# Four weight slots of one 128-column tile and a longer stretch of turns in a hybrid encoder block

## Chip, cores and metric

One core of a Trainium2 chip. The metric is the device time of one execution in microseconds; lower is better. A step, below, is always one expert of one head for 128 tokens (see the kernel).

## Reference

One encoder layer on x of 512 tokens by 2048 features, all in float32, then a final RMSNorm:

```python
h = rmsnorm(x); proj = h @ w_in          # q, k, v, og, two decay gates, glu, ga, gb
yA = (rmsnorm_heads(gla(q, k, v, decay)) * silu(og)) @ w_o
yB = silu(layernorm(depthwise_conv31(glu_in * sigmoid(glu_gate)))) @ w_pw2
x  = x + (sigmoid(ga) * yA + sigmoid(gb) * yB) @ w_out
h2 = rmsnorm(x)                          # PEER: 8 heads, top 16 of 128*128 experts each
x  = x + sum_k softmax_k * gelu(u_tab[idx_k] . h2) * v_tab[idx_k]
```

PEER reads, for each token, head and chosen expert, one row of u_tab and one of v_tab (8 KB each): 512 x 8 x 16 x 2 rows, 1.07 GB. The weights are 16 MiB for each 2048 x 2048 matrix, read once for each group of token blocks that is computed together.

## The kernel before

**Blocks and stages.** The tokens are four blocks of 128. Stage A (to 1303 us of the span) computes the linear attention of all 512 tokens and then everything of block 0 up to its expert indices. Stage B works off the experts of blocks 0 and 1 on VectorE while TensorE does the rest of blocks 1, 2 and 3 beside it. Later stages work off the experts of blocks 2 and 3, with the products of v_tab rows on TensorE.

**Steps.** Stage B is one unrolled list of 256 steps (L1464; 16 units of 16). In each, `dot` (L1301) multiplies a gathered u row with the tokens and `add_row` (L1309) adds a gathered v row, two steps late. GpSimd issues both gathers of a step (L584, L588; 1 MiB each, two buffers for u, four for v) when `dot` and `add_row` free a buffer. ScalarE makes the weight of a step in `expert` (L763). After its dot, each step does its share of the side work in `beside(s)` (L1390 on VectorE, L801 on ScalarE), at step numbers written out by hand (L81 to L101): a piece of side work can't come earlier on VectorE than its step, and a step can't go on until TensorE has delivered what the piece reads.

**Turns.** Steps 0 to 67 carry eight turns, one for each pair of channel tiles (`TURN_AT`, L81): four of ten steps, four of seven. A turn begins with `glu1_take` (L1319), which reads two projections from TensorE, tile by tile (L1327), and then spreads 62 operations of the convolution over its steps (`conv1`, L1332, L1343). In the first four turns TensorE computes four output-gate tiles (`og1`) and the four projections of the next turn (`glu1`), all of 384 columns; in the last four it computes two pairs of gate and value for block 1 (`ma1`, 128 columns) and the next turn's `glu1`. Behind the turns come the gates of the second branch (`GB_AT`, 66), the layer norm (`XC_AT` 71 to `SILU2_AT` 85), the pointwise projection (`PW_AT` 83), the output projection (`RES1_AT` 93 to 99), the second norm (100), and the queries of block 1 (`QUERY1_AT` 105, a head every two steps). From step 130 (`M2_AT`) `merge2` (L1378, L1385) takes a pair of gate and value for blocks 2 and 3 every four steps, 16 times.

**Weights.** SyncE loads them in the order of use with `load` (L484). `wring` has two slots; a load is a slab of 256 output columns, 2 MiB (or two half slabs for v and w_out). Before a load it waits on `w_used`. TensorE waits for the landing in `slab_ready`, computes the slab, and gives the slot back with a drain:

```python
            def slab_used():
                pe.drain().then_inc(w_used, 1)
```

So slab n+2 is issued when slab n has been computed. `tiles` (L1742) computes 2 x 16 matmuls of a slab into one bank, `project` (L1638) 16 matmuls of one tile, `project_out` (L1800) the half slabs of w_out. A float32 matmul shows as two records in the profile.

Of the kernel before, what the change touches and what calls it, by code (L numbers as in the profile page):

```python
# [5 lines left out]
P = 128  # L6
# [8 lines left out]
T = 512  # L15
# [19 lines left out]
WQ, WK, WV, WOG, WGLU, WGATE, WGA, WGB = 0, 4, 8, 16, 24, 32, 40, 48  # L35
OGK = 6144
# [14 lines left out]
SLAB = 4096  # L51
HEAD_SLABS = 4

SB_GLU0 = HEADS * HEAD_SLABS
SB_OG0 = SB_GLU0 + 16
SB_MA0 = SB_OG0 + 8
SB_MB0 = SB_MA0 + 16
SB_OUT0 = SB_MB0 + 16
SB_WQ0 = SB_OUT0 + 8
SB_GLU1 = SB_WQ0 + PH  # L60
SB_OG1 = SB_GLU1 + 2
SB_MA1 = SB_OG1 + 16
SB_MA1_LAST = SB_MA1 + 18
SB_GB1 = SB_MA1_LAST + 4
SB_PW1 = SB_GB1 + 8
SB_OUT1 = SB_PW1 + 8
SB_WQ1 = SB_OUT1 + 8
SB_MA2 = SB_WQ1 + PH
SB_MB2 = SB_MA2 + 16
SB_OUT2 = SB_MB2 + 16  # L70
SB_WQ2 = SB_OUT2 + 8
# [21 lines left out]
QUERY1_AT = 105  # L93
# [51 lines left out]
def hybrid_block(nc, x, norm1_g, w_in, w_gk, gk_f_w, gk_f_b, gk_b_w, gk_b_b, onorm_g, w_o, conv_w, conv_b,  # L145
                 ln_g, ln_b, w_pw2, w_out, norm2_g, w_q, keys, u_tab, v_tab, final_g, out):
    def slab(w, at):

        return w[bass.ds(at, 1)].rearrange("a p f -> p (a f)")

    def half_slab(w, at, s):

        return w[bass.ds(at, 2), :, s * (SLAB // 2):(s + 1) * (SLAB // 2)].rearrange("j p f -> p j f")

    ctx = ExitStack()
    with ctx:
# [25 lines left out]
        wring = sb("wring", [P, 2 * SLAB])  # L182
# [168 lines left out]
        w_in_slot = [sem("w_slot0"), sem("w_slot1")]  # L351
# [104 lines left out]
        def w_slot(n):  # L456

            return view(wring, (n % 2) * SLAB, KT, 256)

        def w_slot_half(n):  # L460

            return view(wring, (n % 2) * SLAB, 2, KT // 2, 256)

        def slot_all(n):

            return wring[:, (n % 2) * SLAB:(n % 2 + 1) * SLAB]

        def slot_halves(n):

            return slot_all(n).rearrange("p (j f) -> p j f", j=2)  # L470

        def by_half(bank):

            return bank.rearrange("p (j c) -> p j c", j=2)


        @block.sync
        def _(sp):
# [5 lines left out]
            def load(n, i, per, dst, src):  # L484

                hold(sp, w_used, i * per + (n + 1), sp_passed)
                sp.dma_start(dst, src).then_inc(w_in_slot[n % 2], 16)

            with sp.Fori(0, HEADS) as h:
                load(0, h, HEAD_SLABS, slot_all(0), slab(w_in, h + WQ))  # L490
                load(1, h, HEAD_SLABS, slot_all(1), slab(w_in, h + WK))
                for s in range(2):
                    load(2 + s, h, HEAD_SLABS, slot_halves(s), half_slab(w_in, h * 2 + WV, s))

            def pair_loads(first, w_gate, o_gate, w_val, o_val):
                with sp.Fori(0, KT // 2) as i:
                    load(first, i, 2, slot_all(0), slab(w_gate, i + o_gate))
                    load(first + 1, i, 2, slot_all(1), slab(w_val, i + o_val))

            def slab_loads(first, w, o, count=PH):  # L500
                with sp.Fori(0, count // 2) as i:
                    for s in range(2):
                        load(first + s, i, 2, slot_all(s), slab(w, i * 2 + (o + s)))

            def out_loads(first):
                with sp.Fori(0, 4) as g:
                    for s in range(2):
                        load(first + s, g, 2, slot_halves(s), half_slab(w_out, g * 2, s))

            pair_loads(SB_GLU0, w_in, WGATE, w_in, WGLU)  # L510
            slab_loads(SB_OG0, w_in, WOG)
            pair_loads(SB_MA0, w_in, WGA, w_o, 0)
            pair_loads(SB_MB0, w_in, WGB, w_pw2, 0)
            out_loads(SB_OUT0)
            slab_loads(SB_WQ0, w_q, 0)

            load(SB_GLU1, 0, 2, slot_all(0), slab(w_in, WGATE))
            load(SB_GLU1 + 1, 0, 2, slot_all(1), slab(w_in, WGLU))
            with sp.Fori(0, 4) as j:
                for s in range(2):  # L520
                    load(SB_OG1 + s, j, 4, slot_all(s), slab(w_in, j * 2 + (WOG + s)))
                load(SB_OG1 + 2, j, 4, slot_all(0), slab(w_in, j + (WGATE + 1)))
                load(SB_OG1 + 3, j, 4, slot_all(1), slab(w_in, j + (WGLU + 1)))
            with sp.Fori(0, 3) as j:
                for a in range(2):
                    load(SB_MA1 + 2 * a, j, 6, slot_all(0), slab(w_in, j * 2 + (WGA + a)))
                    load(SB_MA1 + 2 * a + 1, j, 6, slot_all(1), slab(w_o, j * 2 + a))
                load(SB_MA1 + 4, j, 6, slot_all(0), slab(w_in, j + (WGATE + 5)))
                load(SB_MA1 + 5, j, 6, slot_all(1), slab(w_in, j + (WGLU + 5)))
            for a in range(2):  # L530
                load(SB_MA1_LAST + 2 * a, 0, 4, slot_all(0), slab(w_in, WGA + 6 + a))
                load(SB_MA1_LAST + 2 * a + 1, 0, 4, slot_all(1), slab(w_o, 6 + a))
            slab_loads(SB_GB1, w_in, WGB)
            slab_loads(SB_PW1, w_pw2, 0)
            out_loads(SB_OUT1)
            slab_loads(SB_WQ1, w_q, 0)
# [3 lines left out]
            out_loads(SB_OUT2)  # L540
            slab_loads(SB_WQ2, w_q, 0)
# [418 lines left out]
        def _(dve):  # L960
# [503 lines left out]
            for U in range(2 * PH):  # L1464
                topk = None
                if U >= PH - 1:
                    head = U - (PH - 1)
                    topk = parts_beside(topk_1(head) if head < PH else topk_2(0), 1)
# [117 lines left out]
        def _(pe):  # L1586
# [11 lines left out]
            def slab_ready(n, i=None, per=0):  # L1598

                if i is None:  # L1600
                    pe.wait_ge(w_in_slot[n % 2], 16 * (n // 2 + 1))
                else:
                    pe.wait_ge(w_in_slot[n % 2], i * (8 * per) + 16 * (n // 2 + 1))


            pe.sem_inc(w_used, 2)
# [28 lines left out]
            def project(slot, m, act_in, bank, done, lo=0, hi=T):  # L1635

                for k in range(KT):
                    last = M(ps[bank][:, 0:hi - lo], w_slot(slot)[:, k, m * P:m * P + P], act_in[:, k, lo:hi],  # L1638
                             start=k == 0, stop=k == KT - 1)
                last.then_inc(done, 1)  # L1640
                return last


            with pe.Fori(0, HEADS) as h:
                for s in range(2):
                    slab_ready(s, h, HEAD_SLABS)
                    for m in range(MT):
                        project(s, m, hT, 2 * s + m, q_mm)
                    pe.drain().then_inc(w_used, 1)
# [8 lines left out]
                for s in range(2):  # L1658
                    slab_ready(2 + s, h, HEAD_SLABS)
                    for k in range(KT // 2):  # L1660
                        kk = s * (KT // 2) + k
                        for b in range(NB):
                            last = M(by_half(ps[b][:]), hT[:, kk, b * P:b * P + P], w_slot_half(s)[:, :, k, :],  # L1663
                                     start=kk == 0, stop=kk == KT - 1)
                            if kk == KT - 1:
                                last.then_inc(v_mm, 1)
                    pe.drain().then_inc(w_used, 1)
# [69 lines left out]
            def tiles(slot, act_in, bank, lo, hi, done):  # L1737

                w = hi - lo
                for m in range(2):  # L1740
                    for k in range(KT):
                        last = M(ps[bank][:, m * w:(m + 1) * w], w_slot(slot)[:, k, m * P:m * P + P],  # L1742
                                 act_in[:, k, lo:hi], start=k == 0, stop=k == KT - 1)
                last.then_inc(done, 1)

            def slab_used():
                pe.drain().then_inc(w_used, 1)

            def pairs(name, first, val_in, lo, hi, base=0):
                p = pair[name]  # L1750
                with pe.Fori(0, KT // 4) as i:
                    for m in range(2):
                        pe.wait_ge(p["use"], i * 2 + (base + m + 1))
                        slab_ready(first + 2 * m, i, 4)
                        tiles(0, hT, 4 + 2 * m, lo, hi, p["gate"])
                        slab_used()
                        slab_ready(first + 2 * m + 1, i, 4)
                        tiles(1, val_in, 5 + 2 * m, lo, hi, p["val"])
                        slab_used()
# [3 lines left out]
            def og0_slab(n):  # L1763
                slab_ready(SB_OG0 + n)
                pe.wait_ge(og0["used"], n + 1)
                tiles(n % 2, hT, n % 4, 0, P, og0["mm"])
                slab_used()
# [22 lines left out]
            def project_out(i, first, lhs, nb, bank0, out):  # L1790

                for g in range(2):
                    for s in range(2):
                        slab_ready(first + 2 * g + s, i, 4)
                        for k in range(KT // 2):
                            kk = s * (KT // 2) + k
                            for b in range(nb):
                                if kk == 0:
                                    pe.wait_ge(out["free"], i * (2 * nb) + (g * nb + b + 1))
                                last = M(by_half(ps[bank0 + g * nb + b][:]), lhs(kk, b), w_slot_half(s)[:, :, k, :],  # L1800
                                         start=kk == 0, stop=kk == KT - 1)
# [227 lines left out]
```

## Time and profile before

| | us |
|---|---|
| median of 3 runs | 4702.01 |
| lowest and highest | 4693.57, 4707.21 |
| the profiled execution | 4691.23 |
| its span, first to last instruction | 4689.5 |
| TensorE busy | 3759.9 (80%) |
| VectorE busy | 2744.8 (59%) |
| GpSimd busy | 1409.5 (30%) |
| moved by DMA | 1530.74 MB, mean 326 GB/s |

Durations come from the one profiled execution, whose own time lies 10.8 us under the median. 1.7 us of it lie outside the span. TensorE's granted clock over the span was 0.927 of full speed.

### The profile page before, as it was taken

The numbers are of one execution on the slowest core, as the hardware profiler recorded it, in microseconds if no ns is written. First come the engines' busy times: TensorE is split into PE (matmuls) and PEld (weight loads), VectorE is DVE, ScalarE is ACT, GpSimd is POOL, SyncE is SP. The second block draws the span as 40 slices with busy tenths as digits, with TensorE's granted clock in tenths as the row PEclk, the third lists the DMA queues.
The fourth block names the chain that finished last, engine by engine and source line by source line (L and its number), as shares of the span: only waits on it lengthen the run. The fifth ranks groups of instructions, "written<-read, shape, count | busy, mean of one in ns | idle before, by whom it ended". The sixth has DMA issues, their size and how long they took to land. (4 is left out here: it accounts for less than half of the span.)

```text
span 4689.5 us, 44487 instructions
## 1 busy us (share of the span) xinstructions
PE 3759.9 (80%) x15280; PEld 2396.5 (51%) x15280; DVE 2744.8 (59%) x3996; ACT 873.1 (19%) x2035; POOL 1409.5 (30%) x1038
## 2 busy tenths in 40 slices
PE   6999999999899999767569798730388987677776
PEld 3444459997755576664558686320244443232332
DVE  1332249100589988775667667788857665444544
ACT  1322120100111111242111111011122222212111
POOL 0000000000022212232444445455544555444443
PEclk9999999999999999988789899965699999999999
DMA  2111127677588888999999999998999999999998
GB/s 104 54 72 54 54 90 266 254 268 269 206 340 340 349 351 357 385 404 418 394 404 404 403 418 420 424 354 335 376 422 420 420 398 409 380 419 422 417 422 359
DMA packets 194523, 1530.74 MB, mean 326 GB/s; under 512 B 24280, under 2 KB 30552, under 8 KB 30810
## 3 DMA queue, kind: packets, MB, share of 16 engines
q0 software_dynamic: 147456, 1073.81, 56.4%
q1 hardware_dynamic: 45232, 444.87, 23.9%
q10 hardware_dynamic: 1740, 10.91, 0.6%
q8 instruction: 46, 0.75, 0.1%
q14 instruction: 49, 0.39, 0.0%
HBM read 1525.32 MB, written 4.19 MB: 326 GB/s over the span
## 5 line engine op out<-in xcount | busy, mean ns | idle before, releaser
L584 POOL DMA_INDIRECT arena_c<-in_peer_u,arena_c x320 | 487.6, 1524 | 2488.3 <-issue 1325.2
L1638 PE MATMUL bank<-arena_h,wring 128*128 128x384 f32 (+3 forms) x3200 | 886.5, 440 | 23.8 <-ACT arena_h L731 9.1
L588 POOL DMA_INDIRECT arena_c<-in_peer_v,arena_c x512 | 664.3, 1297 | 642.9 <-PE bank L1950 191.2
L1306 DVE SCALAR_TENSOR_TENSOR arena_c<-arena_c 128x2048 f32<-128x2048 f32 x256 | 585.5, 2287 | 320.3 <-DMA arena_c<-in_peer_u,arena_c 320.3
L1742 PE MATMUL bank<-arena_h,wring 128*128 128x128 f32 (+2 forms) x4608 | 660.9, 305 | 99.9 <-DVE arena_h L1385 53.3
L1638 PEld LDWEIGHTS bank<-arena_h,wring 128*128 128x128 f32 x3200 | 542.1, 197 | 364.5 <-issue 157.4
L1742 PEld LDWEIGHTS bank<-arena_h,wring 128*128 128x128 f32 x4608 | 616.9, 193 | 146.5 <-issue 81.5
L1984 PE MATMUL bank<-arena_c 128*128 128x512 f32 x1024 | 489.1, 627 | 172.1 <-ACT arena_c L932 159.9
L1316 DVE SCALAR_TENSOR_TENSOR arena_o<-arena_c,arena_o 128x2048 f32<-128x2048 f32 x256 | 600.7, 2346 | 6.6 <-ACT arena_c L769 4.1
L1950 PE MATMUL bank<-arena_c 128*128 128x512 f32 x1024 | 483.4, 621 | 114.8 <-ACT arena_c L890 114.7
L1542 DVE SCALAR_TENSOR_TENSOR arena_h<-arena_h,arena_c 128x2048 f32<-128x2048 f32 x128 | 292.8, 2292 | 298.6 <-DMA arena_h<-in_peer_u,arena_c 297.4
L767 ACT ACTIVATE arena_c<-arena_c 128x1 f32<-128x1 f32 x384 | 77.8, 203 | 2077.3 <-DVE arena_c L1306 1625.6
L1984 PEld LDWEIGHTS bank<-arena_c 128*128 128x128 f32 x1024 | 195.3, 199 | 465.8 <-ACT arena_c L932 244.1
L1950 PEld LDWEIGHTS bank<-arena_c 128*128 128x128 f32 x1024 | 198.3, 198 | 366.8 <-issue 233.5
L584 POOL DMA_INDIRECT arena_h<-in_peer_u,arena_c x192 | 255.2, 1329 | 117.4 <-issue 57.0
L1742 PE MATMUL bank<-arena_c,wring 128*128 128x128 f32 (+1 forms) x1536 | 238.7, 318 | 46.5 <-ACT arena_c L707 29.1
L1343 DVE SCALAR_TENSOR_TENSOR arena_c<-arena_c,cols 128x384 f32<-128x384 f32 x480 | 259.5, 608 | 0.0
L1742 PEld LDWEIGHTS bank<-arena_c,wring 128*128 128x128 f32 x1536 | 219.8, 198 | 65.4 <-issue 38.0
L1742 PE MATMUL bank<-arena_o,wring 128*128 128x128 f32 (+1 forms) x1536 | 235.6, 315 | 17.3 <-DMA wring<-in_gla_w_o 15.5
L1825 PE MATMUL bank<-arena_c 128*128 (+1 forms) x128 | 25.1, 339 | 265.0 <-ACT arena_c L738 262.3
L1742 PEld LDWEIGHTS bank<-arena_o,wring 128*128 128x128 f32 x1536 | 216.6, 195 | 36.3 <-DMA wring<-in_gla_w_o 17.7
L1663 PE MATMUL bank<-wring,arena_h 128*128 128x512 f32 x512 | 221.9, 594 | 0.3
(212 smaller groups left out, 2879.9 us busy)
## 6 DMA issues: line engine op xcount, KB each, us to landing
wring<-in_w_in SPq DMA_DIRECT2D x112, 2048.0 KB, 8.3
wring<-in_gla_w_o SPq DMA_DIRECT2D x24, 2048.0 KB, 10.0
wring<-in_conv_w_pw SPq DMA_DIRECT2D x24, 2048.0 KB, 11.2
wring<-in_w_out SPq DMA_DIRECT2D x24, 2048.0 KB, 13.4
wring<-in_peer_w_q SPq DMA_DIRECT2D x24, 2048.0 KB, 11.1
arena_c<-in_peer_v,arena_c POOLq DMA_INDIRECT x512, 11.6
arena_c<-in_peer_u,arena_c POOLq DMA_INDIRECT x320, 10.2
arena_c<-in_x SPq DMA_DIRECT2D x4, 1024.0 KB, 12.7
```

The source lines that it names most:

```text
L584: pool.indirect_dma_start(out=u_rows[s], out_offset=None, in_=u_tab[0], in_offset=at)\
L588: pool.indirect_dma_start(out=v_rows[s], out_offset=None, in_=v_tab[0], in_offset=at)\
L767: A(act_g[:, one], act_u[:, one], ACT.Gelu).then_inc(act_done, 1)
L1306: V.scalar_tensor_tensor(row, row, 1.0, block_of(h2, b), ALU.mult, ALU.mult, accum_out=act_u[:, k:k + 1]).then_inc(u_used, 1)
L1316: V.scalar_tensor_tensor(block_of(x2, b), by_tile(v_row[s]), act_w[:, k:k + 1], block_of(x2, b), ALU.mult, ALU.add).then_inc(v_used, 1)
L1343: ins = V.scalar_tensor_tensor(dst, upad1[:, m, r:r + T1], tap, dst, ALU.mult, ALU.add)
L1542: V.scalar_tensor_tensor(row, row, 1.0, block_of(h2, b), ALU.mult, ALU.mult, accum_out=act_u2[:, m, k:k + 1]).then_inc(u2_used, 1)
L1638: last = M(ps[bank][:, 0:hi - lo], w_slot(slot)[:, k, m * P:m * P + P], act_in[:, k, lo:hi], start=k == 0, stop=k == KT - 1)
L1663: last = M(by_half(ps[b][:]), hT[:, kk, b * P:b * P + P], w_slot_half(s)[:, :, k, :], start=kk == 0, stop=kk == KT - 1)
L1742: last = M(ps[bank][:, m * w:(m + 1) * w], w_slot(slot)[:, k, m * P:m * P + P], act_in[:, k, lo:hi], start=k == 0, stop=k == KT - 1)
L1950: last = M(ps[4 + q][:], diag1[:, k % VS, :], v_row[k % VS][:, q * 512:q * 512 + 512], start=k == 0, stop=k == TOP - 1)
L1984: last = M(ps[4 * m + q][:], diag[:, s, :], v2_row[s][:, q * 512:q * 512 + 512], start=k == 0, stop=k == TOP - 1)
```

## The change

The ring has four slots of one tile of 128 columns (1 MiB) in place of two slabs. A slot is given back by the first matmul of the following tile, with no drain: TensorE adds 3 to `w_used` at the start, and the first matmul of each tile adds 1, so that the load of tile n+3 is issued when the first matmul of tile n is done. v and w_out come as quarters (4 of the 16 row tiles by 512 columns), laid out on the host. The weights' order and their bytes stay. The eight turns take 11, 11, 11, 10, 9, 9, 9 and 8 steps, 78 in all, and what follows up to the queries comes 8 to 10 steps later; `M2_AT` stays at 130. The first search of block 1's indices begins at k = 4 of its unit (`FIND_AT`).

```diff
-TURN_AT = (0, 10, 20, 30, 40, 47, 54, 61, 68)
+TURN_AT = (0, 11, 22, 33, 43, 52, 61, 70, 78)
 OG_AT = (4, 7)
-IT_AT = (2, 4)
-X1_AT = 67
-GB_AT = 66
-XC_AT, SQUARE_AT = 71, 72
-RSTD_AT, ROOT_AT, RECIP_AT = 77, 77, 78
-SCALE1_AT, SILU1_AT = 79, 80
-PW_AT = 83
-SCALE2_AT, SILU2_AT = 84, 85
-RES1_AT = (93, 95, 97, 99)
-NORM1_AT = 100
-QUERY1_AT = 105
+IT_AT = (2, 5)
+X1_AT = 77
+GB_AT = 76
+XC_AT, SQUARE_AT = 81, 82
+RSTD_AT, ROOT_AT, RECIP_AT = 86, 86, 87
+SCALE1_AT, SILU1_AT = 88, 88
+PW_AT = 92
+SCALE2_AT, SILU2_AT = 93, 94
+RES1_AT = (101, 103, 105, 107)
+NORM1_AT = 108
+QUERY1_AT = 113
+FIND_AT = 4
...
-        wring = sb("wring", [P, 2 * SLAB])
+        wring = sb("wring", [P, RING * TILE])
...
-            def load(n, i, per, dst, src):
+            def load(n, i, per, src):
 
                 hold(sp, w_used, i * per + (n + 1), sp_passed)
-                sp.dma_start(dst, src).then_inc(w_in_slot[n % 2], 16)
+                sp.dma_start(slot_all(n), src).then_inc(w_in_slot[n % RING], 16)
...
-            pe.sem_inc(w_used, 2)
+            pe.sem_inc(w_used, RING - 1)
...
-            def project(slot, m, act_in, bank, done, lo=0, hi=T):
+            def project(slot, act_in, bank, lo=0, hi=T, at=0):
 
                 for k in range(KT):
-                    last = M(ps[bank][:, 0:hi - lo], w_slot(slot)[:, k, m * P:m * P + P], act_in[:, k, lo:hi],
+                    last = M(ps[bank][:, at:at + hi - lo], w_tile(slot)[:, k, :], act_in[:, k, lo:hi],
                              start=k == 0, stop=k == KT - 1)
-                last.then_inc(done, 1)
+                    if k == 0:
+                        last.then_inc(w_used, 1)
                 return last
...
-            def slab_used():
-                pe.drain().then_inc(w_used, 1)
+            def two_tiles(first, i, per, act_in, bank, lo, hi):
+
+                for m in range(2):
+                    tile_ready(first + m, i, per)
+                    last = project(first + m, act_in, bank, lo, hi, m * (hi - lo))
+                return last
```

## Rows read from the trace of the kernel before

**Rows 1.** The page: GB/s in 40 equal slices of the span.

```profile
GB/s 104 54 72 54 54 90 266 254 268 269 206 340 340 349 351 357 385 404 418 394 404 404 403 418 420 424 354 335 376 422 420 420 398 409 380 419 422 417 422 359
```

**Rows 2.** Stretches: length, busy us of PE, PEld, DVE, ACT, POOL; clock, DMA share, GB/s.

```profile
1390.00:1477.00 87.00, 85.60 (x264) 49.45 (x263) 80.33 (x101) 15.26 (x32) 22.75 (x20) 1.00 0.88 343
...
1723.00:1801.00 78.00, 72.68 (x384) 54.48 (x383) 65.76 (x88) 12.82 (x24) 14.64 (x13) 0.98 0.84 341
...
1953.00:2455.00 502.00, 333.43 (x1849) 269.45 (x1847) 320.78 (x293) 118.95 (x260) 197.08 (x124) 0.83 0.99 406
```

**Rows 3.** VectorE in time: start, us, operation, [idle before <-releaser]. Dot, add, three projections awaited.

```profile
1303.04 2.29 DVE L1306 SCALAR_TENSOR_TENSOR arena_c<-arena_c 128x2048 f32<-128x2048 f32 x1 [9.07 <-DMA arena_c<-in_peer_u,arena_c]
...
1321.87 2.34 DVE L1316 SCALAR_TENSOR_TENSOR arena_o<-arena_c,arena_o 128x2048 f32<-128x2048 f32 x1
...
1397.66 0.56 DVE L1327 TENSOR_TENSOR arena_c<-bank,arena_c 128x384 f32<-128x384 f32 x1 [6.56 <-PE bank L1638]
...
1722.93 0.56 DVE L1327 TENSOR_TENSOR arena_c<-bank,arena_c 128x384 f32<-128x384 f32 x1 [3.70 <-PE bank L1638]
1733.25 0.56 DVE L1327 TENSOR_TENSOR arena_c<-bank,arena_c 128x384 f32<-128x384 f32 x1 [9.76 <-PE bank L1638]
```

**Rows 4.** TensorE in time, in turns 0, 1 and 4.

```profile
1313.32 20.90 PE L1638 MATMUL bank<-arena_h,wring 128*128 128x384 f32 x64 [0.45 <-issue]
...
1355.71 41.91 PE L1638 MATMUL bank<-arena_h,wring 128*128 128x384 f32 x128 [0.34 <-issue]
1398.34 20.90 PE L1638 MATMUL bank<-arena_h,wring 128*128 128x384 f32 x64 [0.72 <-issue]
...
1680.76 10.20 PE L1742 MATMUL bank<-arena_o,wring 128*128 128x128 f32 x64 [3.05 <-DMA wring<-in_gla_w_o]
1691.30 41.91 PE L1638 MATMUL bank<-arena_h,wring 128*128 128x384 f32 x128 [0.34 <-issue]
```

**Rows 5.** Stretch, as rows 2: four 1 MiB loads of x in line on SyncE's queue.

```profile
3.00:12.00 9.00, 0.00 (x0) 0.00 (x0) 0.00 (x0) 3.90 (x4) 0.38 (x3) 1.00 1.00 409
```

**Rows 6.** VectorE in time: the dot of step 68, merges 0 and 7.

```profile
1952.84 2.27 DVE L1306 SCALAR_TENSOR_TENSOR arena_c<-arena_c 128x2048 f32<-128x2048 f32 x1
...
2459.45 0.69 DVE L1385 TENSOR_TENSOR arena_h<-bank,arena_c 128x512 f32<-128x512 f32 x1
...
2662.15 0.69 DVE L1385 TENSOR_TENSOR arena_h<-bank,arena_c 128x512 f32<-128x512 f32 x1
```

**Rows 7.** TensorE in time: behind the last merge of the turns; first pairs, blocks 2 and 3.

```profile
1927.47 7.41 PE L1742 MATMUL bank<-arena_h,wring 128*128 128x128 f32 x64 [3.10 <-DVE arena_h L1362]
...
2377.49 16.77 PE L1742 MATMUL bank<-arena_h,wring 128*128 128x256 f32 x64 [0.65 <-ACT arena_c L743]
2394.36 14.08 PE L1742 MATMUL bank<-arena_o,wring 128*128 128x256 f32 x64
...
2460.28 16.34 PE L1742 MATMUL bank<-arena_h,wring 128*128 128x256 f32 x64 [23.25 <-DVE arena_h L1385]
```

**Rows 8.** SyncE in time, stage A: two weight loads issued.

```profile
883.75 0.33 SPq L487 DMA_DIRECT2D wring<-in_w_in  x1
891.27 0.33 SPq L487 DMA_DIRECT2D wring<-in_gla_w_o  x1
```

**Rows 9.** DMA issues, 883 to 1003 us: count, KB each, median us to landing.

```profile
wring<-in_w_in SPq DMA_DIRECT2D x8, 2048.0 KB, 7.5
```

**Rows 10.** TensorE in time, stage A: the slab computed behind those loads.

```profile
891.32 7.41 PE L1742 MATMUL bank<-arena_h,wring 128*128 128x128 f32 x64 [0.34 <-DMA wring<-in_w_in]
```

**Rows 11.** Groups of TensorE by shape, 60 to 1303 us: busy, mean ns, idle before.

```profile
L1742 PE MATMUL bank<-arena_h,wring 128*128 128x128 f32 x1536 | 177.5, 276 | 13.4 <-DMA wring<-in_w_in 6.7 <-DVE arena_c L1158 5.3 <-issue 1.4
L1742 PE MATMUL bank<-arena_h,wring 128*128 128x143 f32 x1024 | 130.5, 289 | 6.3 <-issue 2.4 <-DMA wring<-in_w_in 1.7 <-ACT arena_o L661 1.3
...
L1800 PE MATMUL bank<-wring,arena_c 128*128 128x512 f32 x128 | 57.0, 598 | 4.6 <-DMA wring<-in_w_out 2.2 <-DVE arena_c L1162 1.4 <-issue 0.7
```

**Rows 12.** DMA issues as rows 9, beside gathers, 2145 to 2240 us.

```profile
wring<-in_w_out SPq DMA_DIRECT2D x6, 2048.0 KB, 13.8
```

More of the change, by code:

```diff
@@ L350, in hybrid_block @@
         wgk_gap = sem("wgk_gap")
-        w_in_slot = [sem("w_slot0"), sem("w_slot1")]
+        w_in_slot = [sem(f"w_slot{s}") for s in range(RING)]
         w_used = sem("w_used")
@@ L482, in _, with loads @@
                 sp.dma_start(wgk[:, :, 32 * d:32 * d + RANK], w_gk[d]).then_inc(wgk_in, 16)
-            def load(n, i, per, dst, src):
+            def load(n, i, per, src):
                 hold(sp, w_used, i * per + (n + 1), sp_passed)
-                sp.dma_start(dst, src).then_inc(w_in_slot[n % 2], 16)
+                sp.dma_start(slot_all(n), src).then_inc(w_in_slot[n % RING], 16)
+            def loads(n, i, per, w, at, count):
+                for m in range(count):
+                    load(n + m, i, per, piece(w, at + m))
@@ L489, in _ @@
             with sp.Fori(0, HEADS) as h:
[L490 to L493, printed above, removed]
+                loads(0, h, HEAD_TILES, w_in, h * 2 + WQ, 2)
+                loads(2, h, HEAD_TILES, w_in, h * 2 + WK, 2)
+                loads(4, h, HEAD_TILES, w_v, h * 4, 4)
@@ L495, in pair_loads @@
             def pair_loads(first, w_gate, o_gate, w_val, o_val):
                 with sp.Fori(0, KT // 2) as i:
[L497 to L508, printed above, removed]
+                    loads(first, i, 4, w_gate, i * 2 + o_gate, 2)
+                    loads(first + 2, i, 4, w_val, i * 2 + o_val, 2)
+            def row_loads(first, w, o):
+                with sp.Fori(0, KT // 4) as i:
+                    loads(first, i, 4, w, i * 4 + o, 4)
             pair_loads(SB_GLU0, w_in, WGATE, w_in, WGLU)
-            slab_loads(SB_OG0, w_in, WOG)
+            row_loads(SB_OG0, w_in, WOG)
@@ L512, in _ @@
             pair_loads(SB_MA0, w_in, WGA, w_o, 0)
             pair_loads(SB_MB0, w_in, WGB, w_pw2, 0)
[L514 to L518, printed above, removed]
+            row_loads(SB_OUT0, w_out, 0)
+            row_loads(SB_WQ0, w_q, 0)
+            loads(SB_GLU1, 0, 4, w_in, WGATE, 2)
+            loads(SB_GLU1 + 2, 0, 4, w_in, WGLU, 2)
             with sp.Fori(0, 4) as j:
[L520 to L523, printed above, removed]
+                loads(SB_OG1, j, 8, w_in, j * 4 + WOG, 4)
+                loads(SB_OG1 + 4, j, 8, w_in, j * 2 + (WGATE + 2), 2)
+                loads(SB_OG1 + 6, j, 8, w_in, j * 2 + (WGLU + 2), 2)
@@ L524, in _ @@
             with sp.Fori(0, 3) as j:
                 for a in range(2):
[L526 to L529, printed above, removed]
+                    loads(SB_MA1 + 4 * a, j, 12, w_in, j * 4 + (WGA + 2 * a), 2)
+                    loads(SB_MA1 + 4 * a + 2, j, 12, w_o, j * 4 + 2 * a, 2)
@@ L530, in _ @@
+                loads(SB_MA1 + 8, j, 12, w_in, j * 2 + (WGATE + 10), 2)
+                loads(SB_MA1 + 10, j, 12, w_in, j * 2 + (WGLU + 10), 2)
             for a in range(2):
[L531 to L536, printed above, removed]
+                loads(SB_MA1_LAST + 4 * a, 0, 8, w_in, WGA + 12 + 2 * a, 2)
@@ L1792, in project_out @@
                 for g in range(2):
[L1793 to L1796, printed above, removed]
+                    for s in range(4):
+                        tile_ready(first + 4 * g + s, i, 8)
+                        for k in range(QUART):
+                            kk = s * QUART + k
                             for b in range(nb):
```

214 lines of the change are left out of this document (98 added, 116 removed).

## The prediction

> **What bounds the kernel now.** I read the slices first, then a table of stretches, then each engine in order of time at the places that the change touches. The slices [rows 1] show two kernels in one. In stage A, slices 0 to 10, the DMA engines move 54 to 269 GB/s and TensorE sets the pace. From slice 11 on the rate is 340 to 424, and in many slices nothing more goes through: from there on the question is how many bytes are left, and in which stretches the transfers aren't full. The table [rows 2] finds those stretches: in a turn of ten steps 343 GB/s, in a turn of seven 341, behind the turns 406.
>
> Why are the turns not full? VectorE was busy for 80.33 us of the 87 of turn 1, and for 65.76 of the 78 of a short turn [rows 2]. The rest is the wait for the two projections with which a turn begins: 6.56 us at turn 1, and 3.70 + 9.76 at a short turn [rows 3]. TensorE doesn't rest: its records follow each other with gaps of 0.34 and 0.72 us, and from one turn's output gates to the next's it takes 1398.34 - 1313.32 = 85.0 us [rows 4]. So TensorE is the bound of the turns, and VectorE gets through fewer steps beside it than it could. Behind the turns it is the transfers: 99% busy at 406 GB/s [rows 2].
>
> **The added steps in the turns.** A step is a dot and an add, 2.29 + 2.34 = 4.63 us of VectorE [rows 3], and two gathers, 2.10 MB. First four turns, 11, 11, 11 and 10 steps: VectorE needs 80.3 + 4.6 = 85.0 us for eleven, just what TensorE takes for its 128 matmuls. I cost these three steps at nothing; what covers them is the 6.56 us wait, and if TensorE got faster than 85 they would cost up to 4.6 each. Last four, 9, 9, 9 and 8 steps: 65.8 + 2 x 4.6 = 75.0 us against 78. TensorE's own cycle is four slabs of 128 columns and two of 384, 4 x 7.4 [rows 7] + 41.9 = 71.5 us plus the waits for weights, such as 3.05 [rows 4]. The bytes are 12.6 MB of weights and 9 x 2.10 of gathers, 31.5 MB, which at 409 GB/s, the rate that 1 MiB loads reached in line [rows 5], take 77 us. Engines and transfers are then nearly level, so I keep 78 us. The last turn gets one more step, 4.6 us, for part of its own 9.76. Sum: the turns took 1952.8 - 1303.0 = 650 us for 68 steps [rows 3, 6]; I say 652 for 78. Ends: 642, if weight waits and projection waits vanish; 696, if all ten steps are paid with 4.63 us.
>
> **What is left behind the turns.** From step 68 to merge 7 (step 158) took 2662.2 - 1952.8 = 709 us [rows 6], at 406 GB/s [rows 2] 288 MB. Ten steps fewer are 21 MB less, 267 MB. At the same rate that is 657 us, 52 less. If the rate became 424, the best slice [rows 1], 630; this end is 79 less. The other end is that nothing shrinks, because another chain holds it. That chain is TensorE's: gates, layer norm, projections and queries, each released at a step number. From the last merge of the turns (step 65 before, 75 after) to the end of the queries it covers 54 steps before and 52 after, with the same 36 slabs. Before, it ended at 2377.5, and the first pair for blocks 2 and 3 was ready 16.8 + 14.1 = 31 us later, while VectorE asked for it only at 2459.5 [rows 6, 7]: 51 us of lead, seen as TensorE's 23.25 us of waiting after its second pair. After the change the last query is taken at step 127 and merge 0 comes at 130, three steps or some 20 us later, so VectorE waits about 10 us there. The lead is spent. Worked as a chain, from the last merge of the turns (1927.5 us before [rows 7], 2 later now): 450 us to the queries' end, 31 for the pair, and 2662.2 - 2459.5 = 203 for the seven merges behind it give 2613. By bytes: 1303 + 652 + 657 = 2612. Both agree, and merge 7 comes 50 us earlier. What is queued behind a waiting merge 0 on VectorE is the next dot, and behind that the gathers; the two u and four v buffers and the ring keep the transfers going for those 10 us. From merge 7 on both kernels do the same work in the same order.
>
> **The ring in stage A.** One slab is in flight at a time: a load goes out at 883.75, the next at 891.27 when a slab has been computed, landing takes 7.5 us and the slab's matmuls 7.41 [rows 8 to 10]. So TensorE waits 0.34 us for the landing, again and again. The idle time before the weight-fed matmuls of stage A sums to 13.4 + 6.3 + 4.6 = 24.3 us [rows 11], part of it loop branches and waits for VectorE and ScalarE. With three tiles ahead a load has three tiles' time, 11.1 us, to land. I take 15 us off, with 24 as the better end. The other end: each tile now has a wait of its own, and if each of stage A's 176 tiles showed the 0.34 us that a drain with its wait shows [rows 4], while 88 slabs lose it, 30 us come on top. I take the value near the gain, because the row of 41.91 us [rows 4] spans two slabs, a drain and a wait that was met, and shows no gap between them. SyncE issues 416 loads in place of 208 at 0.33 us each [rows 8], against 3.7 us of a tile: hidden. The page "TensorE: Matmul & The Clock Gate" of the Trainium skill (the cost: per-tile semaphore tail) gives each increment about 26.3 ns; by that, an estimate, stage A's additional 88 increments and a few cost 2.3 us or somewhat more, and no run here shows it alone.
>
> **Sum.** Stage A -15, turns +2, behind them -52: -65 us. The profiled execution's 4691 becomes 4626; the median of the runs shown lies 10.8 above it, so the forecast is 4702 - 65 = 4637. Its own range is 4612 to 4664.
>
> **Rivals.** (1) The added steps aren't hidden. TensorE's start of the next projections depends on VectorE having taken the last, and if the 9.76 us between the two tiles [rows 3] stay in each turn while VectorE's work grows, the ten steps cost 46 us. Then 4702 - 15 + 46 - 52 = 4681. Against it: two turns ahead is allowed, TensorE needs only that turn j was taken to finish turn j+1's projections, so a later VectorE finds both ready. 10%.
>
> (2) The chain behind the turns holds. It has two steps fewer, and after each of its stalls three tiles lie ready where four tiles' worth did: 1 MiB at half of 406 GB/s is 5 us, for some five stalls 25 us, with 7 more for a longer wait at merge 0. The 52 shrink to 20: 4669. The 13.8 us to landing beside gathers [rows 12] speak for it, the equal bytes against it. 8%.
>
> (3) Slower: smaller transfers that don't overlap. A slab alone lands in 7.5 us [rows 9]; at 409 GB/s 5.1 of these are bytes and 2.4 are fixed. If the queue worked one load after the other, a tile would take 2.6 + 2.4 = 5.0 us where its matmuls of 128 columns take 3.7. Places: 96 such tiles in stage A (output gates, first and second branch, queries) and 80 in block 1, 176 x 1.3 = 229 us. That is about 4866; it turns the sign once a tile's pitch passes 4.1 us (176 x 0.37 = 65). Against it stands the start of the span: four loads of 1 MiB on one queue moved 409 GB/s with the DMA share at 1.00 [rows 5]. 4%.
> The page "DMA: Bandwidth & Descriptors" of the Trainium skill speaks for this rival: under Bandwidth it lists 6.15 us and 341 GB/s for 1 MB and asks for at least 1 MiB in a transfer, and its fit of 2.0 us plus the bytes at 436 GB/s makes, as an estimate, 4.4 us of a lone tile and 6.8 of a lone slab. By that rule alone a tile in stage A would be loaded 0.7 us slower than it is used.
>
> (4) The change does what it says, but no expected term is there: the turns pay for what the rest wins. 4702 within 14. 6%.
>
> **Chances.** The forecast gets 72%. A measurement here tells 0.3%, 14 us, from no change. Faster takes in the forecast, rival 2 and most of rival 1, 0.88; within 0.3%, the rest of 1, and 4, 0.08; slower is rival 3, 0.04. The range reaches from 4605, where the ends of stage A and of the rate come in part together, to 4682, rival 1.
>
> **What would show it.** The four long turns last 85 us, the wait before L1327 is under 3 us in turns 1 to 7, and the dot of step 78 starts near 1940 (1955 less stage A). The short turns show 390 GB/s or more. In stage A the waits of TensorE for `wring` are gone. TensorE's first pair for blocks 2 and 3 starts near 2360, its wait for merges after the second pair is gone, and VectorE waits once for it, about 10 us; merge 7 comes near 2597. Wrong would be: turns of 83 us or more in the short ones; a landing of a tile above 5 us in stage A with waits for it; or a stretch behind the turns below 400 GB/s.

## The result, and the profile after

The median went from 4697.79 us (4 runs, 4687.07 to 4707.21) to 4581.31 us (4 runs, 4576.65 to 4583.68): a ratio of 0.9753, 95% interval 0.9734 to 0.9771, 116 us less. The forecast was 4637, and its range ended at 4605. The profiled execution took 4576.65 us, its span is 4573.9, 115.6 less than the span before.

The page after, GB/s in 40 slices; it answers to [rows 1]:

```profile
GB/s 115 47 64 64 46 84 290 261 301 292 214 365 375 368 414 417 397 406 424 412 406 425 408 425 413 387 359 321 409 412 423 422 397 412 380 414 422 418 418 361
```

The slices are shorter now and full sooner: 414 GB/s from the fifteenth, where before it took until the nineteenth to reach 418. The stretches of the kernel after, in the columns of [rows 2]: two long turns, two short ones, from the turns to merge 0's first wait, and the merges:

```profile
1345.00:1430.00 85.00, 85.00 (x265) 50.03 (x264) 84.89 (x104) 15.76 (x34) 25.44 (x22) 1.00 0.96 372
1430.00:1515.00 85.00, 85.00 (x265) 50.10 (x264) 84.89 (x105) 15.77 (x34) 25.46 (x22) 1.00 0.96 368
1674.00:1750.00 76.00, 72.25 (x400) 54.72 (x400) 74.72 (x96) 13.82 (x28) 20.34 (x18) 1.00 1.00 417
1750.00:1826.00 76.00, 72.23 (x400) 54.70 (x399) 74.89 (x96) 13.81 (x28) 20.61 (x18) 1.00 1.01 422
1896.00:2321.00 425.00, 282.91 (x1658) 226.38 (x1658) 277.79 (x264) 112.67 (x239) 178.61 (x104) 0.86 1.00 413
2321.00:2540.00 219.00, 205.88 (x954) 180.89 (x953) 148.67 (x160) 42.17 (x84) 91.21 (x56) 0.97 0.99 412
```

In a long turn TensorE and VectorE are both busy for all of the 85 us; VectorE had idled 6.6 of 87. In a short one VectorE is busy for 74.7 and 74.9 of 76 us, and the transfers go from 341 GB/s to 417 and 422.

TensorE in stage A, in order of time, first before and then after; these lines answer to [rows 10]:

```profile
899.37 7.41 PE L1742 MATMUL bank<-arena_o,wring 128*128 128x128 f32 x64 [0.64 <-DMA wring<-in_gla_w_o]
907.50 7.41 PE L1742 MATMUL bank<-arena_h,wring 128*128 128x128 f32 x64 [0.71 <-DVE arena_c L1158]
915.01 7.41 PE L1742 MATMUL bank<-arena_o,wring 128*128 128x128 f32 x64
922.76 7.41 PE L1742 MATMUL bank<-arena_h,wring 128*128 128x128 f32 x64 [0.34 <-DMA wring<-in_w_in]
930.27 4.95 PE L1742 MATMUL bank<-arena_o,wring 128*128 128x128 f32 x42
```

```profile
894.97 7.31 PE L1627 MATMUL bank<-arena_o,wring 128*128 128x128 f32 x64
902.11 7.31 PE L1627 MATMUL bank<-arena_h,wring 128*128 128x128 f32 x64
909.26 7.31 PE L1627 MATMUL bank<-arena_o,wring 128*128 128x128 f32 x64
916.41 7.31 PE L1627 MATMUL bank<-arena_h,wring 128*128 128x128 f32 x64
923.55 7.31 PE L1627 MATMUL bank<-arena_o,wring 128*128 128x128 f32 x64
```

Slabs followed each other every (930.27 - 899.37) / 4 = 7.73 us. Now no idle time is left, and two tiles follow two tiles every (923.55 - 894.97) / 4 = 7.15 us; the list of TensorE's waits of stage A has none for `wring` any more. VectorE at the first dot, at the second projection of turn 0 and both of the second short turn, at step 78's dot and at merges 0 and 7, for [rows 3, 6]:

```profile
1253.51 2.29 DVE L1295 SCALAR_TENSOR_TENSOR arena_c<-arena_c 128x2048 f32<-128x2048 f32 x1 [6.75 <-DMA arena_c<-in_peer_u,arena_c]
...
1265.34 0.56 DVE L1316 TENSOR_TENSOR arena_c<-bank,arena_c 128x384 f32<-128x384 f32 x1 [8.98 <-PE bank L1627]
...
1676.45 1.01 DVE L1316 TENSOR_TENSOR arena_c<-bank,arena_c 128x384 f32<-128x384 f32 x2
...
1896.28 2.27 DVE L1295 SCALAR_TENSOR_TENSOR arena_c<-arena_c 128x2048 f32<-128x2048 f32 x1
...
2333.54 0.69 DVE L1374 TENSOR_TENSOR arena_h<-bank,arena_c 128x512 f32<-128x512 f32 x1 [10.30 <-PE bank L1627]
...
2541.70 0.68 DVE L1374 TENSOR_TENSOR arena_h<-bank,arena_c 128x512 f32<-128x512 f32 x1
```

The wait for projections is left in turn 0 alone (8.98 us; 65.2 us in all turns before). In the second short turn both tiles lie ready and stand in one line without an idle time.

From such starts of dots every run below is cut into four parts: stage A to the first dot, the turns to the dot behind them (step 68 or 78), from there to the dot of step 158 (that of merge 7), and the rest. In us:

| | stage A | turns | to step 158 | rest | span |
|---|---|---|---|---|---|
| before (68 steps) | 1303.0 | 649.8 | 707.1 | 2029.5 | 4689.5 |
| after (78 steps) | 1253.5 | 642.8 | 643.2 | 2034.4 | 4573.9 |
| forecast | -15 | +2 | -52 | 0 | -65 |
| measured | -49.5 | -7.0 | -63.9 | +4.9 | -115.6 |

Each part is read from one profiled execution. Where their code is the same, stage A took 1253.5, 1254.1, 1254.7 and 1259.4 us in the kernel after and in three runs below, and the rest took 2028 to 2038 us in all runs but one. So differences of up to some 6 us in one part of one run aren't read as effects here, and the +4.9 is of that size.

The eight turns one by one, from dot to dot, four long and four short ones. In us, with the two kernels of the first experiment beside them:

| | 0 | 1 | 2 | 3 | 4 | 5 | 6 | 7 |
|---|---|---|---|---|---|---|---|---|
| before | 85.2 | 87.1 | 85.0 | 84.9 | 71.6 | 79.4 | 78.5 | 78.1 |
| after | 91.7 | 84.9 | 84.9 | 80.3 | 78.8 | 76.0 | 75.8 | 70.3 |
| ring alone, old steps | 86.9 | 84.9 | 82.6 | 82.5 | 68.0 | 72.3 | 72.5 | 72.2 |
| new steps, old ring | 90.4 | 87.1 | 85.2 | 80.3 | 84.4 | 82.1 | 80.2 | 78.5 |

### The profile page after: what moved, and what is told of

The parts are those of the page before. It is cut to its first block and busy times, and to the rows that moved or that the text cites. A ratio compares the mean times of both kernels' runs of the same rounds, so it can differ in the third digit from the quotient of the medians.

```text
span 4573.9 us, 45320 instructions
## 1 busy us (share of the span) xinstructions
PE 3703.6 (81%) x15280; PEld 2382.4 (52%) x15280; DVE 2743.7 (60%) x3996; ACT 873.1 (19%) x2034; POOL 1411.1 (31%) x1038
## 5 line engine op out<-in xcount | busy, mean ns | idle before, releaser
L1627 PE MATMUL bank<-arena_h,wring 128*128 128x128 f32 (+4 forms) x7808 | 1521.8, 358 | 64.3 <-DVE arena_h L1351 20.8
L573 POOL DMA_INDIRECT arena_c<-in_peer_u,arena_c x320 | 499.5, 1561 | 2368.7 <-issue 1272.5
L1531 DVE SCALAR_TENSOR_TENSOR arena_h<-arena_h,arena_c 128x2048 f32<-128x2048 f32 x128 | 292.6, 2291 | 298.8 <-DMA arena_h<-in_peer_u,arena_c 297.5
L573 POOL DMA_INDIRECT arena_h<-in_peer_u,arena_c x192 | 235.7, 1228 | 117.2 <-issue 56.5
L1651 PE MATMUL bank<-wring,arena_h 128*128 128x512 f32 x512 | 220.8, 593 | 0.0
L1778 PE MATMUL bank<-wring,arena_h 128*128 128x512 f32 x384 | 175.1, 615 | 46.6 <-DVE arena_h L1377 25.1
L1476 DVE SCALAR_TENSOR_TENSOR arena_h<-arena_h,arena_c 128x2048 f32<-128x2048 f32 x64 | 146.6, 2292 | 97.1 <-DMA arena_h<-in_peer_u,arena_c 91.0
```

Of the source, the lines that this page charges most:

```text
L573: pool.indirect_dma_start(out=u_rows[s], out_offset=None, in_=u_tab[0], in_offset=at)\
L1476: V.scalar_tensor_tensor(row, row, 1.0, block_of(h2, b), ALU.mult, ALU.mult, accum_out=act_u[:, k:k + 1]).then_inc(u2_used, 1)
L1531: V.scalar_tensor_tensor(row, row, 1.0, block_of(h2, b), ALU.mult, ALU.mult, accum_out=act_u2[:, m, k:k + 1]).then_inc(u2_used, 1)
L1627: last = M(ps[bank][:, at:at + hi - lo], w_tile(slot)[:, k, :], act_in[:, k, lo:hi], start=k == 0, stop=k == KT - 1)
L1651: last = M(ps[b][:], hT[:, kk, b * P:b * P + P], w_quart(s)[:, k, :], start=kk == 0, stop=kk == KT - 1)
L1778: last = M(ps[bank0 + g * nb + b][:], lhs(kk, b), w_quart(s)[:, k, :], start=kk == 0, stop=kk == KT - 1)
```

## The experiments

### Each part alone

```diff
 # e1_ring_old_steps: the kernel after, with
-TURN_AT = (0, 11, 22, 33, 43, 52, 61, 70, 78)
+TURN_AT = (0, 10, 20, 30, 40, 47, 54, 61, 68)
...
-FIND_AT = 4
+FIND_AT = 1
 # e2_steps_old_ring: the kernel before, with the step numbers of the kernel after
```

> The changed kernel with the step numbers of before (68 steps in the turns, first search at k = 1): the ring alone. Theory S, the two parts add up: stage A ends where the changed kernel's does, 49 us early; the turns are bound by the same TensorE work and win only the drains, some 10 us; behind them the transfers are full either way, 0 to 10. Total 60 to 70 us less, near 4633. Rival, the ring brings nearly all of it and the steps nothing: 105 us or more less, near 4590.

> The kernel before with the new step numbers (78 steps in the turns, first search at k = 4) and its ring of two slabs with drains: the steps alone. Theory S: stage A unchanged, turns of 650 to 660 us for 78 steps, 45 to 55 us less behind them: near 4648. Rival, the steps need the ring (weights late beside more gathers): the four short turns take 84 us or more and less than 25 us remain, near 4675.

| | median (runs) | ratio to before, 95% | stage A | turns | to step 158 | rest |
|---|---|---|---|---|---|---|
| ring alone, 68 steps | 4608.74 (4) | 0.981, 0.979 to 0.983 | 1254.1 | 621.9 | 696.0 | 2032.1 |
| steps alone, 78 steps | 4661.34 (4) | 0.9925, 0.9901 to 0.9949 | 1304.0 | 668.3 | 651.2 | 2031.4 |

The kernel before had a median of 4694.70 beside both, so the ring alone brings 86 us, the steps alone 33, and the sum is 119, near the change's 116. That they add up held; how they divide did not: 4609 was measured for the ring where 4633 was expected, and 4661 for the steps, between the expected 4648 and its rival's 4675. The ring takes 28 us out of the turns where 10 were expected. The steps win 707.1 - 651.2 = 56 us behind the turns (45 to 55 were expected), but they cost 18.5 in the turns; with the ring it is 52.8 against 20.9. The ring also carries the new layout of v and w_out, which no run takes apart from it. TensorE in a short turn, in order of time, first the ring alone, then the steps with the old ring:

```profile
1675.22 7.31 PE L1627 MATMUL bank<-arena_o,wring 128*128 128x128 f32 x64
1682.37 7.31 PE L1627 MATMUL bank<-arena_h,wring 128*128 128x128 f32 x64
1689.51 3.74 PE L1627 MATMUL bank<-arena_o,wring 128*128 128x128 f32 x32
1694.14 3.84 PE L1627 MATMUL bank<-arena_o,wring 128*128 128x128 f32 x32 [0.90 <-DMA wring<-in_gla_w_o]
1699.07 48.69 PE L1627 MATMUL bank<-arena_h,wring 128*128 128x384 f32 x192 [1.09 <-DMA wring<-in_w_in]
```

```profile
1748.81 9.04 PE L1743 MATMUL bank<-arena_o,wring 128*128 128x128 f32 x64 [3.95 <-DMA wring<-in_gla_w_o]
1758.19 7.41 PE L1743 MATMUL bank<-arena_h,wring 128*128 128x128 f32 x64 [0.34 <-issue]
1769.83 9.04 PE L1743 MATMUL bank<-arena_o,wring 128*128 128x128 f32 x64 [4.23 <-DMA wring<-in_gla_w_o]
1779.21 41.91 PE L1639 MATMUL bank<-arena_h,wring 128*128 128x384 f32 x128 [0.34 <-issue]
```

With slabs, a wait of about 4 us comes twice in a turn, and the matmuls behind it take 9.04 us for 7.41. These 1.63 us are the clock, in two stretches behind the first of these waits (length, busy us of PE, granted clock, DMA share, GB/s):

```profile
1751.80:1753.50 1.70, 1.70 (x10) 0.51 1.02 419
1753.50:1757.80 4.30, 4.30 (x39) 1.00 0.99 419
```

TensorE idled for 3.95 us, and behind that the granted clock was 0.51 for a while, its lower level of 1.2 GHz, and then 1.00 again. So these late weights cost their wait and 1.63 us more. With tiles the same weights are late by 0.9 and 1.1 us, and the matmuls take 7.31 for two tiles, at full clock. Short turns of seven steps took 68.0 to 72.5 us with the ring (71.6 to 79.4 before), and of nine steps with slabs 80.2 to 84.4.

### The drains

```diff
 # e4_ring_with_drains: the kernel after, with a drain behind every second tile (e5: behind each)
+            def slab_end(m):
+                if m % 2 == 1 or False:
+                    pe.drain()
...
 # e3_slabs_no_drain: the kernel before, slabs given back by the next one's first matmul
-            pe.sem_inc(w_used, 2)
+            pe.sem_inc(w_used, 1)
...
+                    if m == 0 and k == 0:
+                        last.then_inc(w_used, 1)
...
-                pe.drain().then_inc(w_used, 1)
+                return
```

> The kernel before, with its slabs and its step numbers, but a slab is given back by the first matmul of the next one and there is no drain. In a stretch of slabs without stalls the loads go out at the same moments as before. Theory D, the drains were what stage A lost: 35 us or more less in stage A, and slabs of 128 columns follow each other in 7.5 us or less on average in place of 7.7. Theory L, the landing of one slab at a time was what it lost: under 10 us less in stage A. Behind stage A either could lose some 10 us to the shorter lead after stalls.

> The changed kernel with a drain after every second tile, where the slabs ended; loads, slots and step numbers stay. Theory D: 35 to 45 us of stage A's gain go again, tiles of 128 columns take 7.5 us or more a pair in place of 7.15. Theory L: less than 10 us go. In the turns, where TensorE and VectorE are level, D expects 1 to 2 us a turn; behind them nothing, since the transfers are full.

> The changed kernel with a drain after every tile, twice as many as with a drain after every second tile (there stage A took 36.3 us more, 0.41 us for each of 88). Theory D, a drain has a fixed price: stage A 72 us over the changed kernel's 1253.5, near 1326. Rival, the price was that of the slabs' bank changes and loop branches: under 50 us more.

| | median (runs) | ratio to before, 95% | stage A | turns | to step 158 |
|---|---|---|---|---|---|
| ring, a drain behind every second tile | 4613.68 (4) | 0.9823, 0.9800 to 0.9846 | 1289.8 | 648.0 | 643.2 |
| ring, a drain behind each tile | 4663.19 (2) | 0.9933, 0.9913 to 0.9952 | 1324.0 | 658.8 | 645.7 |
| slabs, no drain | 4775.81 (4) | 1.0168, 1.0146 to 1.0189 | 1326.3 | 655.3 | 746.5 |

The drain stands in the program so that a slot is given back only when its slab's matmuls are done. In stage A it has a fixed price: 88 of them cost 1289.8 - 1253.5 = 36.3 us, 176 cost 70.5, so 0.41 and 0.40 us each. That is theory D, and 36 of stage A's 49.5. In the turns 40 drains cost 5.2 us, less than the 1 to 2 us a turn that were expected, and behind them nothing (643.2 both times): there VectorE and the transfers set the time. TensorE in stage A, in order of time, with a drain behind every second tile:

```profile
895.47 7.41 PE L1627 MATMUL bank<-arena_o,wring 128*128 128x128 f32 x64
903.55 7.41 PE L1627 MATMUL bank<-arena_h,wring 128*128 128x128 f32 x64 [0.67 <-DVE arena_c L1147]
911.06 7.41 PE L1627 MATMUL bank<-arena_o,wring 128*128 128x128 f32 x64
918.77 7.41 PE L1627 MATMUL bank<-arena_h,wring 128*128 128x128 f32 x64 [0.30 <-issue]
926.29 7.41 PE L1627 MATMUL bank<-arena_o,wring 128*128 128x128 f32 x64
```

Two tiles now take (926.29 - 895.47) / 4 = 7.70 us in place of 7.15, but the idle times printed beside the four intervals sum to 0.97 us, where 2.2 are lost. The lines 911.06 and 926.29 print none: their gaps are 911.06 - (903.55 + 7.41) = 0.10 us and 0.11, which this view leaves out. The other half of the loss, 1.1 us, stands in the durations: 7.41 for 7.31, and records that no longer overlap, as they did at 7.31 us every 7.15. All of stage A, without and with these drains (length, busy us of PE, PEld, DVE, ACT, POOL; clock, DMA share, GB/s):

```profile
60.00:1253.50 1193.50, 1151.58 (x5969) 793.79 (x5968) 387.25 (x1093) 210.64 (x360) 3.92 (x4) 1.00 0.46 161
60.00:1289.80 1229.80, 1173.19 (x5965) 797.81 (x5964) 387.52 (x1093) 210.06 (x360) 3.92 (x4) 0.99 0.44 157
```

Of the 36.3 us, 1173.19 - 1151.58 = 21.6 show as busy time of TensorE and 14.7 as idle time.

The lines look like those before: waits of 0.67 and 0.30 us stand where 0.71 and 0.34 stood with slabs, although three tiles are ahead. So the 0.34 us that the prediction read as waiting for the landing were in the main the drain's.

The slabs without drains went the other way than both theories said: 23 us more in stage A, 81 in all. So in the kernel before, the drain wasn't the only thing that held a slab. TensorE there, in order of time:

```profile
901.45 7.41 PE L1744 MATMUL bank<-arena_o,wring 128*128 128x128 f32 x64 [0.63 <-DMA wring<-in_gla_w_o]
909.61 7.41 PE L1744 MATMUL bank<-arena_h,wring 128*128 128x128 f32 x64 [0.74 <-DMA wring<-in_w_in]
917.67 7.41 PE L1744 MATMUL bank<-arena_o,wring 128*128 128x128 f32 x64 [0.65 <-DMA wring<-in_gla_w_o]
925.77 7.41 PE L1744 MATMUL bank<-arena_h,wring 128*128 128x128 f32 x64 [0.70 <-DMA wring<-in_w_in]
```

A slab every 8.1 us: 7.4 to 7.5 for the landing [rows 9], and 0.7 because the load goes out only when the slab's first matmul is done (SyncE issues at 902.18 and 910.34, with slabs started at 901.45 and 909.61). With one slab in flight the landing is a second bound, nearly as high as the 7.73 us of the slab with its drain. Taking the drain away alone gives nothing, and behind the turns the kernel loses 39 us more, where the smaller lead after stalls is the likely cause; no run shows it alone. The expectation also held that the loads would go out at the same moments, and they did not: this run doesn't separate the drain from the landing as it was meant to, and the division rests on the two runs with drains.

### The lead

```diff
 # e6_two_tiles_ahead: the kernel after, with  (e7_one_tile_ahead: RING - 3)
-            pe.sem_inc(w_used, RING - 1)
+            pe.sem_inc(w_used, RING - 2)
 # e8_drain_gives_back: the kernel after, with
-            pe.sem_inc(w_used, RING - 1)
+            pe.sem_inc(w_used, RING)
...
-                    if k == 0:
-                        last.then_inc(w_used, 1)
...
+            def slab_end(m):
+                pe.drain().then_inc(w_used, 1)
...
```

> The changed kernel with two tiles ahead in place of three (2 added to the slots' count at the start in place of 3). Theory R, the ring's gain outside the drains is lead: in stage A a load has 7.3 us to land in place of 11, and needs about 5, so stage A stays within 2 us; beside the gathers, where a landing takes longer, it is late: the four short turns rise from 76 to 80 us or more, and the part behind the turns loses 10 us or more. Rival, the lead doesn't matter once the drains are gone: everything within 5 us of the changed kernel.

> The changed kernel with one tile ahead. A load then has one tile's time, 3.6 us at 128 columns. If a lone 1 MiB load takes 5.0 us to land (2.6 for the bytes and 2.4 fixed, worked out from the slab's 7.5), stage A's 96 tiles of 128 columns take 5.0 to 5.6 us in place of 3.57: 140 to 190 us more in stage A. If small loads were no slower for their bytes than large ones (3.75 us a tile), it would be under 30 us more.

> Four tile slots, each given back by a drain after its own tile, so that four tiles are ahead in a stall in place of three; drains as in the run with a drain after each tile. Theory R: stage A as in that run, near 1326; in the turns and behind them no later than there, up to 15 us earlier because of the fourth tile after stalls. Rival, the three tiles' lead is enough: the same as that run within 5 us behind stage A.

| | median (runs) | ratio to before, 95% | stage A | turns | to step 158 |
|---|---|---|---|---|---|
| three tiles ahead (after) | 4581.31 (4) | 0.9753, 0.9734 to 0.9771 | 1253.5 | 642.8 | 643.2 |
| two | 4599.80 (4) | 0.9802, 0.9785 to 0.9820 | 1255.0 | 650.1 | 655.3 |
| one | 5254.34 (2) | 1.1192, 1.1169 to 1.1214 | 1546.1 | 747.9 | 834.2 |
| four, by drains | 4665.30 (4) | 0.9941, 0.9924 to 0.9957 | 1321.0 | 656.5 | 642.2 |

Two tiles are enough where nothing else moves (1.5 us in stage A, not told from none), and beside the gathers the third is worth 7.3 + 12.1 us, 18 by the medians. The last three short turns took 78.7, 79.3 and 74.8 us in place of 76.0, 75.8 and 70.3; 80 or more had been expected. The fourth is worth 2 to 4 us a part against the run with a drain behind each tile: nothing that the medians tell (4665 and 4663). With one tile ahead the landing time that rival 3 worked out appears. TensorE and the loads' landing in stage A:

```profile
963.67 3.84 PE L1627 MATMUL bank<-arena_o,wring 128*128 128x128 f32 x32 [0.40 <-DMA wring<-in_gla_w_o]
969.15 3.84 PE L1627 MATMUL bank<-arena_o,wring 128*128 128x128 f32 x32 [1.65 <-DMA wring<-in_gla_w_o]
974.68 3.84 PE L1627 MATMUL bank<-arena_h,wring 128*128 128x128 f32 x32 [1.69 <-DMA wring<-in_w_in]
```

```profile
wring<-in_w_in SPq DMA_DIRECT2D x14, 1024.0 KB, 4.7
```

A lone load of 1 MiB lands in 4.7 us (5.0 had been worked out), and the tile's pitch is 5.5. Stage A grew by 293 us where 140 to 190 were expected. The sum had only the 96 tiles of 128 columns, and for these it was right: 182 us, busy and idle together. It left out the 32 tiles of 143 columns, 59 us, and the quarters of w_out, 47; the quarters of w_v, with 512 columns to compute, aren't late. Two groups of stage A (busy, mean ns, idle before):

```profile
L1651 PE MATMUL bank<-wring,arena_h 128*128 128x512 f32 x512 | 220.8, 593 | 0.0
L1627 PE MATMUL bank<-arena_h,wring 128*128 128x143 f32 x1024 | 137.9, 295 | 47.3 <-DMA wring<-in_w_in 46.1 <-ACT arena_o L650 1.3
```

The page "DMA: Bandwidth & Descriptors" of the Trainium skill gives, by its fit of 2.0 us plus the bytes at 436 GB/s, 4.4 us for such a load, as an estimate. The fit is for loads that GpSimd issues, and here SyncE issues them; the trace's 4.7 is near it.

### The turns taken apart, and two tries

```diff
 # e10_ring_drains_old_steps: drains behind every second tile and the 68 steps of before
 # e9_merges_two_steps_later
-M2_AT = P + 2
-X2_AT = P + 32
-RES2_AT = (P + 68, P + 72, P + 76, P + 80)
-NORM2_AT = P + 81
+M2_AT = P + 4
+X2_AT = P + 34
+RES2_AT = (P + 70, P + 74, P + 78, P + 82)
+NORM2_AT = P + 83
 # e11_merge_one_step_earlier
-IT_AT = (2, 5)
+IT_AT = (2, 4)
```

> The four-slot ring with 68 steps in the turns and a drain after every second tile: what the lead brings in the turns without the drains' removal. The ring without drains took 621.9 us for these turns, the kernel before 649.8. A long turn has four drains and a short one six, 0.40 us each by the runs with drains: theory, the turns take 16 us more than without drains, near 638, and the remaining 12 us are waits for weights in the short turns. Stage A near 1290. Rival, the lead is all of it: the turns stay within 4 us of 622.

> The changed kernel with the merges of blocks 2 and 3, their residual and the second norm two steps later (merge 0 at step 132). VectorE's one wait for the first pair, 10.3 us at merge 0, should go. Theory B, bytes set this part: the transfers were at 389 GB/s around it where 425 is full, so no more than 3 us can be won, and the total is the same within 5 us. Rival, the wait is on the path: 8 to 10 us less.

> The changed kernel with the second merge of each short turn back at its fourth step instead of the fifth. TensorE waits 20.8 us for the last of these merges; a step of these turns is some 8.5 us, so the wait falls to about 12. Theory B: the transfers are full there (414 GB/s or more), so the total stays within 5 us. Rival, the chain behind the turns starts there and all of it comes 8 us earlier.

| | median (runs) | ratio to before, 95% | stage A | turns | to step 158 |
|---|---|---|---|---|---|
| ring with drains, 68 steps | 4649.83 (4) | 0.9890, 0.9875 to 0.9905 | 1288.5 | 637.1 | 693.0 |
| merges two steps later | 4575.09 (5) | 0.9736, 0.9723 to 0.9750 | 1254.7 | 644.9 | 641.6 |
| merge one step earlier | 4580.06 (5) | 0.9743, 0.9730 to 0.9756 | 1259.4 | 644.1 | 642.7 |

The ring's 27.9 us in the turns are 15.2 of drains (637.1 - 621.9; 16 were expected) and 12.7 of lead. Behind the turns the ring with drains has the same gain as without, 14 and 11 us: that part is lead alone.

With the merges two steps later, the wait of 10.3 us is gone from VectorE's list of waits, and the waits for gathers there rise. From 2270 to 2420 us (us in total, times, longest), first the kernel after, then the try:

```profile
DVE arena_c L1295 <- DMA arena_c<-in_peer_u,arena_c: 41.6, 15, 4.7
DVE arena_h L1374 <- PE bank L1627: 10.5, 2, 10.3
```

```profile
DVE arena_c L1295 <- DMA arena_c<-in_peer_u,arena_c: 48.4, 19, 4.4
```

Of 10.5 us 7 come back as waits for rows of u_tab. The two ratios differ by 0.0017, 8 us, but their intervals overlap, so the totals alone leave both the theory and its rival open; what speaks for the theory is the trace. The earlier merge took TensorE's wait from 20.8 to 7.4 us (12 were expected). From the first dot to step 158 the kernel after took 1286.0 us, and the two tries 1286.5 and 1286.8. Both traces speak for the bytes as what sets the time behind the turns.

## Why the prediction was wrong

**The bound.** Right: the turns were TensorE's, and what lies behind them the transfers'. VectorE's wait for projections went, but for the 8.98 us of turn 0; the rate in short turns rose to 417 and 422 GB/s; merge 0 waits 10.3 us, where about 10 were forecast. None of the three signs of being wrong appeared, but the places in time that it gave came 44 to 56 us early: step 78 at 1896 for 1940, TensorE's first pair at 2304 for 2360, merge 7 at 2542 for 2597. What failed are the sizes of three terms, and they miss 51 us together: stage A 34.5, the turns 9, behind them 12, and 5 the other way in the rest.

**"I take 15 us off, with 24 as the better end".** This is the first term that failed, and the largest: stage A won 49.5. The step was to take TensorE's idle time before the weight-fed matmuls as the most that could be won, and to price the drain by that column: the row of 41.91 us was read as a sign that a drain inside it costs nothing. The 24.3 us weren't all of that column, either; with the groups of tiles that the sum left out it is 37.2 us, and 10.2 after, 27 won. A drain costs 0.40 us in stage A, 36 us for 88, and 21.6 of these aren't in the idle column at all. The remaining 13 us, between 1303.0 and the ring with drains, are near the 14.6 us for which the trace before waits for landings in stage A. The page "TensorE: Matmul & The Clock Gate" of the Trainium skill bears on it: under step-by-step it says that the end of one matmul overlaps the start of the next, so that a stream pays only for its columns; its section on a single matmul's latency gives, for bf16, the constant that a lone one shows as 166 to 183 ns. By 88 such constants, an estimate, it is 16 us; measured were 36, more than twice that for each drain. The 2.3 us of increments, by its section on the semaphore tail, which is about small matmuls packed into the array, aren't seen: the stream with an increment in each tile shows no gap, at 7.15 us for two tiles. No run leaves the increments out.

**"So I keep 78 us" for a short turn.** The second: the nine-step turns took 78.8, 76.0 and 75.8, and the ring alone made the last three seven-step turns 72.3. The weight waits in the short turns were put at their size of before, 3.05 us and the like, and no term took them off for the ring; it was priced in stage A only. Drains and lead are worth 27.9 us in all eight turns. Against that, "I cost these three steps at nothing" and the two hidden steps of each short turn were too low: the ten steps cost 20.9 us with the ring and 18.5 with slabs, as much as 4.5 steps of pure VectorE time. In the long turns it is 4.9 us with the ring, nearly all of it in turn 0, and 0.8 with slabs: without drains TensorE needs less than 85 us for a long turn (82.5 with ten steps), which the prediction named as the point from which a step has a price. In the short turns it is 16.0 and 17.6; with the ring VectorE is then busy for nearly all of the turn, and with slabs the weights are late. That -7 came out near the forecast +2 is luck: two errors, of -28 and +19 us, almost cancel.

**"At the same rate that is 657 us, 52 less".** For the steps it was right, 52.8 with the ring and 56 without. What lacks is the ring again: 8 to 11 us, by a rate that rose from 406 to 413 GB/s, which the forecast held for fixed. With two tiles ahead this part takes 12.1 us more and the rate is 405, so it is the lead that brings it.

**The rivals.** That the steps aren't hidden (46 us) came in part, 20.9, though not by the wait between the two tiles that it named. The chain behind the turns didn't hold. That 1 MiB loads don't overlap had the landing time nearly right, 5.0 for 4.7 us, and a condition that isn't met: with three tiles ahead stage A has no wait for weights. Where it is met, with one ahead, the kernel takes 673 us more, three times the rival's 229. What the forecast did not have among its rivals is the ring as more than a remedy for 24 us.

## To carry to other kernels

Price a drain, or anything that breaks a stream of matmuls, from the distance between starts with and without it, and not from the idle column: here it was 0.40 us each in stage A, where TensorE sets the pace. The kernel before has 208 of them; put into the ring, all together cost 32 us (4614 and 4581), because elsewhere they are hidden. A change of a buffer ring acts wherever the ring is used, so its term has to be worked out in every stage, with the late landings of that stage. And a wait that is taken off an engine gave nothing that these runs can tell where the transfers were full; steps moved into a stretch whose transfers aren't full win their bytes (here 5 us each) less what they cost there (2).

## What was not expected of the hardware

- In stage A a drain costs 0.40 to 0.41 us of TensorE's time, the same at 88 and at 176 of them, and 21.6 of 36.3 us show as busy time, not as idle time.
- Behind a wait of 3.95 us for weights the granted clock was 0.51 for a while, and 64 records took 9.04 us in place of 7.41.
- Two tiles of 1 MiB ahead are enough to hide the 2 us by which a lone one lands later than its bytes need (stage A +1.5 us with two tiles ahead, +293 with one).
- A DMA share of 1.00 doesn't tell the rate: it stood beside 409 GB/s [rows 5], 413 and 417, and 1.01 beside 422.
